# A fused two-block transformer kernel: chunk evictions issued ahead of the background work, sliding-window heads in pairs, sigmoid in two steps, convolution every fourth half

## Time and profile before

| | us |
|---|---|
| median of 3 runs | 2651.42 (2647.84 to 2651.52) |
| the profiled execution | 2651.17 |
| its span, first to last instruction | 2649.4 |
| around the span | 1.8 |

### The profile page before, as it was taken

One profiled execution on the slowest core, in us unless ns is written; L12 is line 12 of the kernel. 1 busy time (PEld: TensorE's weight loads), 2 busy tenths in 40 slices (PEclk: granted clock), 3 DMA queues, 4 the chain that ended last, 5 costly groups with the idle time before them and its releaser, 6 DMA issues.

```text
span 2649.4 us, 31358 instructions
## 1 busy us (share of the span) xinstructions
PE 2606.3 (98%) x12478; PEld 2161.0 (82%) x12478; DVE 1615.8 (61%) x1978; ACT 1364.9 (52%) x1940; POOL 0.2 (0%) x4
## 2 busy tenths in 40 slices
PE   9999999999999999999899999999999999999998
PEld 7877888888888887887788888888888888888887
DVE  7685555555555556568788865644555555555555
ACT  6554544444444446578879654544444444444444
POOL 0000000000000000000000000000000000000000
PEclk9999999999999999999999999999999999999999
DMA  6533665566656654654454346544565565555554
GB/s 222 169 135 126 223 191 192 189 191 191 191 187 186 190 191 152 197 176 152 124 173 143 128 135 226 184 148 141 177 204 190 185 190 192 186 186 191 192 189 143
DMA packets 235528, 468.69 MB, mean 177 GB/s; under 512 B 8219, under 2 KB 17654, under 8 KB 234102
## 3 DMA queue, kind: packets, MB, share of 16 engines
q1 hardware_dynamic: 234246, 465.11, 53.7%
q10 hardware_dynamic: 1136, 1.58, 0.2%
HBM read 460.36 MB, written 6.29 MB: 176 GB/s over the span
## 4 chain that ended last, share of the span: by engine, by line
PE 48%; DVE 1%; ACT 1%; DMA 1%; issue 0%; DVEq 0%; ACTq 0%
PE ps L168 46%; PE ps L172 2%; DMA Wt<-in_w_out 1%; DVE XS L138 0%; DVE WL L138 0%; ACT PRD L135 0%; DVE AC L138 0%; ACT WH L135 0%; DVE H L138 0%; DVE FO L145 0%; DVE QA L149 0%; ACT JK L135 0%; DVE H L149 0%; DVE QE L149 0%; DVE QA L138 0%
## 5 line engine op out<-in xcount | busy, mean ns | idle before, releaser
L138 DVE TENSOR_TENSOR WL<-Wt,WH 128x1024 fp32r<-128x1024 f32 (+2 forms) x863 | 1041.7, 1209 | 800.3 <-ACT WH L135 743.1
L135 ACT ACTIVATE WH<-Wt 128x1024 fp32r<-128x1024 f32 (+2 forms) x863 | 899.1, 1045 | 797.3 <-PE ps L168 789.8
L168 PE MATMUL ps<-WH,XT 128*128 128x512 f32 (+1 forms) x3392 | 1085.1, 393 | 0.3 <-DVE XT L138 0.3
L168 PE MATMUL ps<-WH,HT 128*128 128x512 f32 (+2 forms) x3392 | 1061.0, 389 | 3.9 <-DVE WL L138 3.9
L168 PEld LDWEIGHTS ps<-WH,HT 128*128 128x128 f32 x3392 | 636.7, 189 | 129.8 <-DVE WL L138 4.8
L168 PEld LDWEIGHTS ps<-WH,XT 128*128 128x128 f32 x3392 | 636.1, 188 | 130.4 <-issue 2.6
L168 PE MATMUL ps<-WL,XT 128*128 128x512 f32 (+1 forms) x1696 | 658.0, 388 | 0.0
L168 PE MATMUL ps<-WL,HT 128*128 128x512 f32 (+2 forms) x1696 | 655.4, 386 | 0.0
L168 PEld LDWEIGHTS ps<-WL,HT 128*128 128x128 f32 x1696 | 320.0, 189 | 61.4 <-issue 1.0
L168 PEld LDWEIGHTS ps<-WL,XT 128*128 128x128 f32 x1696 | 319.0, 188 | 61.9 <-issue 1.0
L138 DVE TENSOR_TENSOR H<-H,ps 128x512 f32<-128x512 f32 x144 | 92.8, 683 | 23.3 <-PE ps L168 23.3
(11 more groups left out here) (263 smaller groups left out, 1274.1 us busy)
## 6 DMA issues: line engine op xcount, KB each, us to landing
Wt<-in_mlp_w SPq DMA_DIRECT2D x128, 1024.0 KB, 5.3
Wt<-in_w_up SPq DMA_DIRECT2D x64, 1024.0 KB, 5.6
Wt<-in_w_down SPq DMA_DIRECT2D x64, 1024.0 KB, 5.0
Wt<-in_w_in SPq DMA_DIRECT2D x53, 1024.0 KB, 5.1
Wt<-in_w_out SPq DMA_DIRECT2D x32, 1024.0 KB, 5.0
Wt<-in_xa_wk SPq DMA_DIRECT2D x16, 1024.0 KB, 5.0
Wt<-in_xa_wv SPq DMA_DIRECT2D x16, 1024.0 KB, 5.1
Wt<-in_xa_wq SPq DMA_DIRECT2D x16, 1024.0 KB, 5.0
```

The costliest lines, as they stand in the source:

```text
L135: return self.p.act.do(lambda e: e.activation(out, in_, func, **kw), w, self.name + "_a")
L138: return self.p.dve.do(lambda e: e.tensor_tensor(out, a, b, op), w, self.name + "_v")
L168: return self.p.pe.do(lambda e: e.matmul(out, l, r, start=start, stop=stop), w, self.name + "_t" if sig else None)
```

## The change

Evictions: in `gemm` the eviction of a chunk is issued behind the matmuls of its last half and ahead of the pump of that half; the pump then takes only the generators that were there before. The last GEMM, evicted by blocks, is as before. Order of the projections: q0, q1, q2, kv0, kv1, kv2, kv3; the MLA heads join at kv1 (the fifth, as before). SWA: heads are taken in pairs of one parity (the bias columns and sinks are reordered for it once, by small copies); a pair's six score matmuls go to two banks; one ScalarE copy of 128 x 512 brings the first bank to SBUF, a copy_predicated of 2 x 128 brings in the second a step later, one scalar_tensor_tensor of 128 x 512 scales and adds the bias, and one reduce of 4 x 128 takes the maximum. A group has 10 steps instead of 9; the second generator starts three steps behind. `sigm_steps` yields once more, between Abs and Exp. `pace` starts at 3. `gen_o` yields once more before its transposes.

```diff
--- before.py
+++ after.py
@@ -293,9 +293,9 @@
     gfree = [[None, None], [None, None]]
     bg = []
 
-    def pump():
-        for g in list(bg):
-            if next(g, "end") == "end":
+    def pump(running=None):
+        for g in list(bg) if running is None else running:
+            if g in bg and next(g, "end") == "end":
                 bg.remove(g)
 
     def finish_bg():
@@ -366,7 +366,10 @@
                         st_g.mm(o, xh, wl, start=False, stop=False, sig=False)
                         tok = st_g.mm(o, xl, wh, start=False, stop=stop, sig=last)
                 pe_free[i] = tok
-                pump()
+                running = list(bg)
+                if last_seg and k2 == kb - 2 and not ends:
+                    gfree[gs] = evac(ci, c0, w, [G[gs][tb][:, 0:w] for tb in range(2)], tok)
+                pump(running)
             if ends:
                 i = state["half"]
                 split_to(i + NR - 1)
@@ -384,8 +387,6 @@
                         tok = st_g.mm(o, xl, wh, start=False, stop=(kt == kb - 1), sig=(kt == kb - 1))
                     evac.block(ci, c0, w, tb, o, tok)
                 return tok
-            if last_seg:
-                gfree[gs] = evac(ci, c0, w, [G[gs][tb][:, 0:w] for tb in range(2)], tok)
         return tok
 
     def cols(a, b):
@@ -393,7 +394,7 @@
 
     up_chunks = [[(e * 1024, 512), (e * 1024 + 512, 512)] for e in range(8)]
     add_gemm("w_in", A["w_in"], (0, KT), [(1024, 512), (1536, 512), (2048, 320), (0, 512), (512, 512)])
-    QKV = ["q0", "q1", "kv0", "kv1", "q2", "kv2", "kv3"]
+    QKV = ["q0", "q1", "q2", "kv0", "kv1", "kv2", "kv3"]
     for key in QKV:
         c = 512 * int(key[-1])
         add_gemm(key, A["w_q_b" if key[0] == "q" else "w_kv_b"], (0, 4), [(c, 512)])
@@ -427,6 +428,7 @@
     GR2 = arena("GR2", [P, 3, P], 60928)
     PI = arena("PI", [P, 2 + 256], 62464, I32)
     RBF = arena("RBF", [P, 64], 63552)
+    RBP = inht("RBP", [P, 64], 30976)
     RB1 = arena("RB1", [P, 2, 64], 63808)
     PR = arena("PR", [2, P], 64320, I32)
     GR3 = arena("GR3", [3, P], 64832)
@@ -537,8 +539,10 @@
         t_pr = st0.copy(GR3[0:2, :], PR[0:2, :], t_misc)
         t_pf.append(st0.copy(PF[:, 2:258], PI[:, 2:258], t_misc))
         t_idb.append(st0.copy(IDB[:, :], ident, t_c))
-        a = st0.copy(RBB[:, 0, :], RBF[:, :], t_rb)
-        b = st0.tt(RB1[:, 0, :], RBF[:, :], RBB[:, 0, :], SUB, a)
+        a = [st0.copy(RBP[:, :].rearrange("p (g o i) -> p g o i", o=2, i=2)[:, :, odd, :],
+                      RBF[:, :].rearrange("p (g i o) -> p g i o", i=2, o=2)[:, :, :, odd], t_rb) for odd in range(2)]
+        a = st0.copy(RBB[:, 0, :], RBP[:, :], a)
+        b = st0.tt(RB1[:, 0, :], RBP[:, :], RBB[:, 0, :], SUB, a)
         yield
         bi, bk, bf = banks.get()
         t = st0.tr(bk[:, 0:3], GR3[0:3, :], ident[0:3, 0:3], t_pr, bf)
@@ -804,7 +808,7 @@
     KTD = inh("KTD", [P, 2, 256], 8192)
     PTS2 = [[inh(f"PTS0{i}", [P, 2, 3, P], 10240 + 3072 * i) for i in range(2)],
             [arena("PTS10", [P, 2, 3, P], 68096), inht("PTS11", [P, 2, 3, P], 28672)]]
-    S = arena("S", [P, 2, 2, 4, P], 59904)
+    S = arena("S", [P, 2, 2, 2, 2, P], 59904)
     t_win = [None]
     tok_q, tok_kv = {}, {}
     t_kr, t_swa = [None], [None]
@@ -857,45 +861,68 @@
             banks.free(bi, t_q[pr])
             if pr % 2:
                 yield
+        for odd in range(2):
+            t_sink.append(st.copy(SINK2.rearrange("p (g o i) -> p g o i", o=2, i=2)[:, :, odd, :],
+                                  SINK[:, :].rearrange("p (g i o) -> p g i o", i=2, o=2)[:, :, :, odd], t_late))
         for _ in rr(swa_heads(0, t_q, t_k), swa_heads(1, t_q, t_k)):
             yield
         t_swa[0] = [tok_y[13], tok_y[15]]
+
+    SINK2, t_sink = small(16), []
 
     def swa_heads(par, t_q, t_k):
         st = Stage(p, f"swa{par}")
         mx, ms, es, sm_, rd = (small(8) for _ in range(5))
-        s_free = pt_free = t_free = None
+        s_free = pt_free = None
         PTS = PTS2[par]
         spare = [t_cols, t_rbb, t_pf, t_col0, t_bias[0], [n_in.sq, tok_x]]
         if par:
-            for _ in range(4):
+            for _ in range(3):
                 yield
-        sb = S[:, par, :, :, :]
-        v = sb.rearrange("p b h k -> p (b h) k")
+        sb = S[:, par, :, :, :, :]
+        v = sb.rearrange("p o i b k -> p (o i b) k")
         for hg in (par, par + 2):
             g = hg // 2
-            ready = []
-            for i in range(4):
-                h = 4 * hg + i
-                pb, tile = (h % 2) * 64, h // 2
-                bi, bk, bf = banks.get()
-                q0 = QST[pb:pb + 64, tile, :]
-                kk = KTD[pb:pb + 64, g, :]
-                st.mm(bk[:, 0:128], q0[:, 0:128], kk[:, 0:128], t_q[tile // 2], t_k, bf, sig=False)
-                t = st.mm(bk[:, 128:384], q0[:, 128:256], kk[:, 0:256])
-                a = st.stt(sb[:, 0, i, :], bk[:, 0:128], 0.125, BIAS[:, h, 0, :], MUL, ADD, t, spare, s_free)
-                b = st.stt(sb[:, 1, i, :], bk[:, 128:256], 0.125, BIAS[:, h, 1, :], MUL, ADD)
-                c = st.stt(TMP[:, par, :], bk[:, 256:384], 0.125, BIAS[:, h, 1, :], MUL, ADD, t_free)
-                t_free = d = st.pred(sb[:, 1, i, :], cst("ge").bitcast(I32), TMP[:, par, :], b, c)
-                banks.free(bi, c)
-                ready += [a, d]
-                if i % 2:
-                    yield
-            sk = SINK[:, 4 * hg:4 * hg + 4].unsqueeze(1).to_broadcast([P, 2, 4])
-            m3 = mx.rearrange("p (b h) -> p b h", b=2)
-            a = st.red(mx, v, MAX, ready)
-            a = st.tt(m3, m3, sk, MAX, a, t_late)
-            c = st.tt(ms.rearrange("p (b h) -> p b h", b=2), sk, m3, SUB, a)
+            ge2 = cst("ge").bitcast(I32).unsqueeze(1).to_broadcast([P, 2, P])
+
+            def scores(odd):
+                (b0, k0, f0), (b1, k1, f1) = banks.get(), banks.get()
+                for i in range(2):
+                    pb, tile = odd * 64, 2 * hg + i
+                    q0 = QST[pb:pb + 64, tile, :]
+                    kk = KTD[pb:pb + 64, g, :]
+                    for o, qs, ks in ((k0[:, 2 * i * P:(2 * i + 1) * P], 0, 0),
+                                      (k0[:, (2 * i + 1) * P:(2 * i + 2) * P], 1, 0),
+                                      (k1[:, i * P:(i + 1) * P], 1, 1)):
+                        t = st.mm(o, q0[:, qs * P:(qs + 1) * P], kk[:, ks * P:(ks + 1) * P], t_q[tile // 2], t_k,
+                                  f0, f1, sig=(i == 1 and ks == 1))
+                c = st.act(sb[:, odd, :, :, :].rearrange("p i b k -> p (i b k)"), k0, ACT.Copy, t, spare, s_free)
+                banks.free(b0, c)
+                return b1, k1, t, c
+
+            def masked(odd, b1, k1, t, c):
+                d = st.pred(sb[:, odd, :, 1, :], ge2, k1[:, 0:256].rearrange("p (h k) -> p h k", h=2), c, t)
+                banks.free(b1, d)
+                o = sb[:, odd, :, :, :].rearrange("p i b k -> p (i b k)")
+                bias = BIAS[:, 4 * hg + 2 * odd:4 * hg + 2 * odd + 2, :, :].rearrange("p i b k -> p (i b k)")
+                return st.stt(o, o, 0.125, bias, MUL, ADD, d, t_bias[0])
+
+            def largest(odd, d):
+                return st.red(mx[:, 4 * odd:4 * odd + 4], v[:, 4 * odd:4 * odd + 4, :], MAX, d)
+
+            sc = scores(0)
+            yield
+            d = masked(0, *sc)
+            sc = scores(1)
+            yield
+            e, d = d, masked(1, *sc)
+            top = [largest(0, e)]
+            yield
+            top.append(largest(1, d))
+            sk = SINK2[:, 4 * hg:4 * hg + 4].unsqueeze(2).to_broadcast([P, 4, 2])
+            m3 = mx.rearrange("p (h b) -> p h b", b=2)
+            a = st.tt(m3, m3, sk, MAX, top, t_sink)
+            c = st.tt(ms.rearrange("p (h b) -> p h b", b=2), sk, m3, SUB, a)
             b = st.ts(mx, mx, -1.0, MUL, a)
             yield
             e2 = st.act(es, ms, ACT.Exp, c)
@@ -913,7 +940,7 @@
             for tb in range(2):
                 bi, bk, bf = banks.get()
                 for i in range(4):
-                    t = st.tr(bk[:, i * P:(i + 1) * P], sb[:, tb, i, :], ident, n, bf, sig=(i == 3))
+                    t = st.tr(bk[:, i * P:(i + 1) * P], sb[:, i % 2, i // 2, tb, :], ident, n, bf, sig=(i == 3))
                 for i in range(2):
                     bv = bk[:, 256 * i:256 * i + 256].rearrange("p (h q) -> p h q", h=2)
                     if tb == 0:
@@ -1047,7 +1074,7 @@
     bg.append(chain(gen_prep(), gen_bias(), gen_swa()))
     t_win[0] = gemm("w_in", xt, tok_x, ev_win)
     for key in QKV:
-        if key == "q2":
+        if key == "kv1":
             bg.extend(gen_mla(i) for i in range(8))
         gemm(key, lambda part, kt, o=0 if key[0] == "q" else 4: CT[:, part, o + kt, :],
              tok_c[0 if key[0] == "q" else 1], ev_tok(key))
@@ -1177,7 +1204,7 @@
     tok_z = [[t_zz, qa_free], [t_zz, qa_free]]
     t_ga, t_cp = {}, [None] * 8
```

(2 more changed lines are left out.)

## The result

The changed kernel takes 2643.92 us (median of 17 runs, 2641.94 to 2646.82) against 2651.1 for the kernel before in the same sitting (17 runs, 2647.23 to 2653.95): a ratio of 0.9973, 95% interval 0.9967 to 0.9980, or 7.2 us less. The forecast was 2634: the direction and the range held, the gain was forecast over twice too large.

What follows compares the result with a forecast made beforehand. TensorE's own work was taken as the bound (2606.3 of 2649.4 us busy). Terms -9.5 - 2.1 - 1.8 - 3.8 - 5.5 + 1.0 + 0.3 + 4.0 = -17.4 took 2651.2 to 2634; own range 2627 to 2642, wider range 2622 to 2648.

Steps and rivals of the forecast that it cites:

- the flush pump: End of SWA, one pump later, so the loop behind the projections pumps twice: 0 to 2 us, taken as +0.3.
- what comes back: TensorE is through sooner while VectorE and ScalarE keep almost the same work, so delays reach it more often: +4, bounds 0 and +9.
- q, k and v, the waits and the clock: All five QB waits go (-9.5); half clock after QB waits goes, there (-2.1) and in the next stretch (-1.8).
- rival A: Eviction first holds the ScalarE and VectorE queues at a chunk's last half: +8.5 us, near 2643; chance 0.20.
- TensorE's own additions: SWA: three score matmuls a head for two, 16 more instructions over the same columns; +1 us, bounds 0 and 5.2.
- SWA's waits: SWA: 7.7 us less VectorE work shortens the CT and PTS waits and the half clock: -5.5, bounds 0 and -10.1.
- Narrow chunks: Last v chunk and narrow ones: WH 2.2 us earlier removes the 2.09 us WL wait; with other gaps and clock, -3.8.
- Convolution: Pace 3 moves three groups from q, k, v to the delta rule; three halves of cover left at w_out_2: 0.
- The rest: Eviction first elsewhere: the MLP has no gap and the H waits lie two halves behind the eviction, so 0.
- the turn of o: Near the end, it goes from half 513 to 514 and is needed at 518: 0.
- B: Gaps only move to other waits in these stretches; 20 of 22.7 us of gains come back: 2648; chance 0.14.
- C: SWA: a pair's second bank, read a step later, makes TensorE wait for banks; slower, about 2659; chance 0.06.

## Why the prediction was right and wrong

The forecast was -17.4 us and the two profiles differ by 7.6. The 9.8 us between them, by where the halves begin: 6.8 up to the end of SWA (-4.2 forecast with TensorE's additions and the flush pump, +2.6 measured), 2.6 in q, k and v (-13.4, -10.8), 3.2 in the narrow chunks (-3.8 and the +4 for what comes back, +3.4), and -2.8 behind them (0, -2.8).

**q, k and v, the waits and the clock (-9.5, -2.1, -1.8 = -13.4).** Right in mechanism and nearly in size: 10.8 us between halves 384 and 428. All five QB waits went, and no clock drop is left in the stretch; 2.6 came back as the wait for QA. But the step credited two edits together. The sigmoid alone does it. The eviction's place, which rival A priced at +8.5, costs 4 to 5 us in the changed kernel and is worth nothing on the kernel before. A was right that the eviction holds what is behind it in the queue, but the loss is not at an engine standing idle: it is at PTS and QA, wanted sooner than the evicted chunk.

**TensorE's own additions (+1, bounds 0 and 5.2).** The step that failed: "matmuls overlap and the columns are the same". It measured +5.4. What changed was not the count but where neighbours lie, in partitions and in banks. The mean of 322 ns in the earlier trace rows was no price for one of them: eight take 0.93 us in the timeline, not 2.6, since neighbours overlap. That the overlap hung on where they lie was in no row of before, and the timeline of the pair would have been the place to ask. The Trainium skill, "TensorEngine Tiling (Array Packing)", section "Key Properties", says that tiles operate independently and different ones can load weights and multiply in parallel; its section "Restrictions and Gotchas" adds that different row tiles write to different PSUM banks. The trace agrees with the first, 0.93 us for 1.57; the second no run here tests by itself. The prediction did not weigh that rule.

**SWA's waits (-5.5, bounds 0 and -10.1).** CT's wait went, and in the two profiles the gaps are 0.4 us and the clock 3.1 us less, so -3.5. But the old attention code has a clock of 0.98 too in the profile with the sigmoid alone, with the wait for CT still there, so the 3.1 us cannot be put down to the change. PTS waits 4.0 us, 2.0 without KV's eviction ahead of it, and in the old attention code 2.5 or 3.3 by the profile. With the +5.4 above, the stretch ends later than before. VectorE's saving is 7.5 us in its own groups, as worked out, and putting the old heads back costs nothing: the waits left are set by what lies ahead in the queue. This step failed too: a lighter VectorE was taken to shorten the waits.

**Narrow chunks (-3.8).** Wrong in sign: +3.4. The wait for WL went as said. The step left out was who is late next: TensorE, no longer held back, ran into the gates' matmul, 6.3 us, with 5.1 us of work at half clock. "What comes back" (+4) was meant for this, but as a spread over all stages with no place; in its place it was mainly one wait.

**Convolution (0).** Wrong as a price: 3 to 4.5 us. The four ScalarE instructions and the addition that a pump loses are work ahead of WH and QE. The forecast counted this work (5.1 and 3.7 us less) but gave the change no gain for it. The cover at w_out_2 held, as said: no wait for HT.

**Projections and the flush pump (+0.3).** The 2.6 us at half 54 are 1.0 from before half 20 and 5.4 - 3.5 of SWA, which leaves nothing that can be told for this; it was not tried alone. Nor was the order of the projections.

**The rest (0).** The MLP has no gap, as said. Of the 2.8 us, 0.6 lie in halves 446 to 510, 1.8 in 518 to 540 and 0.4 behind them. The 1.8 are w_out_2, where two waits for H (line 149, 1.5 us in all) are gone. These waits stand in the profiles of the three kernels without the later turn of o (the kernel before, only the eviction first, only the sigmoid) and in none of the eleven with it, whichever of the other parts they have. So the turn of o, forecast at 0, seems to be worth these 1.8 us; no run changed it alone.

Of the rivals, A had the right time (2643) by luck: its own cost measured 4 to 5 us for the 8.5 it named, half of the 10 us that were missing, and the dearer score matmuls and the narrow chunks made up the rest. The clock drops did not all follow a gap of over 2 us, as the prediction had it: the one at 1321 us came behind two waits of 1.5 and 1.6. And B's own sum gives 2649.8 with the +1.3 of TensorE's additions and the flush pump, not 2648. B holds for the eviction alone (QE and PTS in QB's place) and for the narrow chunks, not for the sigmoid. C did not happen in the changed kernel; its mechanism was shown where both banks of a pair are held across a step.

## What to carry to other kernels

Where one engine's queue feeds the weights of the next half, a run of long passes ahead of that feed should be cut into steps before anything else is tried: here one `yield` gave the whole gain. Moving an instruction first in a queue moves all others back, so ask for each who waits soonest; the chunk's eviction had two halves of slack and PTS had none. When a wait is removed, walk the engine forward to its next small dependency and give that one slack too, and look at whether neighbouring matmuls over 64 partitions overlap in the timeline. Alternating the halves, with a bank for each, saved 5.4 us of TensorE's time here but none of the kernel's, so look at the waits behind it first.

## What the runs showed that was not expected

Two neighbouring heads' fp32 score matmuls over 64 partitions take 0.93 us when they lie in opposite halves of the partitions with banks of their own (23 of the 24 such pairs in the profiles of the kernel before, of the old heads put back and of the opposite halves; one took 1.48), and 1.57 to 1.60 when they lie in the same half and share banks, be it eight records or twelve. And a work stream cut to a slower pace, with the same work in all, was worth 3 to 4.5 us on engines busy for four fifths of the time. Last, at equal gaps the granted clock fell in one execution and not in another, so that some 2 us of a stretch can be the execution's and not the kernel's.
